# The last layer of a two-block model taken for its 256 real tokens instead of all 272

## What is computed

```python
h = jnp.concatenate([meta, x], axis=1)                      # 16 + 256 positions
...
def _diff_attend(qb, q_pos, kh, vh, k_pos, lam):
    s = jnp.einsum('bhcqd,bhckd->bhcqk', qb, kh)
    mask = k_pos[None, :] <= q_pos[:, None]
    p = jax.nn.softmax(jnp.where(mask, s, -jnp.inf), axis=-1)
    pd = p[:, :, 0] - lam * p[:, :, 1]
    return jnp.einsum('bhqk,bhkv->bhqv', pd, vh)
...
h = h + _diff_attn(hn, c_w_in[j], c_lambda[j], c_subln[j], c_w_out[j], lambda_init)
h = h + _sq_relu_mlp(_rmsnorm_2(h, norm_mlp[layer]), mlp_w1[layer], mlp_w2[layer])
...
h = _rmsnorm_2(h, norm_final)
return h[:, N_META:, :]
```

## Time and profile before

| | us |
|---|---|
| time, median of 3 runs | 2396.36 |
| lowest and highest of them | 2395.44, 2396.42 |
| span of the profiled execution | 2395.3 |
| PE busy in it | 2356.0 |
| DVE busy | 1701.0 |
| ACT busy | 1346.7 |

### The profile page before, as it was taken

How to read it: one execution, slowest core, us unless ns; L and a number is a source line. 1 busy time by engine, 2 the same in 40 slices (tenths; PEclk the granted TensorE clock), 3 DMA queues, 4 the chain that set the end, 5 groups by cost and what they waited for, 6 DMA issues and landing times.

```text
span 2395.3 us, 55555 instructions
## 1 busy us (share of the span) xinstructions
PE 2356.0 (98%) x20019; PEld 2260.4 (94%) x20019; DVE 1701.0 (71%) x3359; ACT 1346.7 (56%) x2806; POOL 3.4 (0%) x9
## 2 busy tenths in 40 slices
PE   8999999999999999999999999999999999999998
PEld 8899999789999999999998999999899999999998
DVE  7667667877658788776586677667666775677865
ACT  5555556365555555565555555557755454566443
POOL 0000000000000000000000000000000000000000
PEclk9999999999999999999999999999999999999999
DMA  6535665335654444456655356654444555434554
GB/s 240 176 118 169 195 204 167 96 110 181 204 177 133 138 134 140 141 167 193 201 165 178 124 167 193 201 172 151 140 129 143 167 177 178 130 112 142 176 183 132
DMA packets 103409, 385.88 MB, mean 161 GB/s; under 512 B 11345, under 2 KB 13521, under 8 KB 103025
## 3 DMA queue, kind: packets, MB, share of 16 engines
q1 hardware_dynamic: 102784, 381.78, 50.6%
q0 software_dynamic: 496, 2.38, 0.3%
HBM read 383.07 MB, written 1.05 MB: 160 GB/s over the span
## 4 chain that ended last, share of the span: by engine, by line
PE 87%; DVE 7%; ACT 3%; issue 2%; DMA 0%; DVEq 0%; ACTq 0%; SPq 0%
PE acc L533 25%; PE acc L540 24%; PE acc L539 24%; DVE weights_lo L2189 2%; PE acc L751 1%; PE acc L753 1%; PE acc L752 1%; ACT weights_hi L1334 1%; PE acc L773 1%; DVE h L2348 1%; DVE y L2337 1%; PE acc L840 1%; DVE xn_parts L2344 1%; PE acc L863 1%; PE acc L885 1%
## 5 line engine op out<-in xcount | busy, mean ns | idle before, releaser
L2189 DVE TENSOR_TENSOR weights_lo<-weights,weights_hi 128x512 fp32r<-128x512 f32 (+1 forms) x1160 | 754.4, 681 | 333.6 <-ACT weights_hi L1334 329.9
L1334 ACT ACTIVATE weights_hi<-weights 128x512 fp32r<-128x512 f32 (+1 forms) x1160 | 673.4, 618 | 189.7 <-PE acc L540 160.9
L533 PE MATMUL acc<-xn_parts,weights_hi 128*128 128x256 f32 (+1 forms) x2560 | 730.3, 285 | 8.7 <-DVE weights_lo L2189 7.1
L540 PE MATMUL acc<-xn_parts,weights_lo 128*128 128x256 f32 (+1 forms) x2560 | 719.4, 281 | 0.0
L539 PE MATMUL acc<-xn_parts,weights_hi 128*128 128x256 f32 (+1 forms) x2558 | 718.8, 281 | 0.0
L533 PEld LDWEIGHTS acc<-xn_parts,weights_hi 128*128 128x128 f32 x2560 | 482.2, 188 | 20.5 <-issue 10.7
L533 PE MATMUL acc<-arena_r,weights_hi 128*128 128x256 f32 (+1 forms) x1760 | 497.3, 283 | 3.0 <-DVE weights_lo L2189 1.7
L540 PE MATMUL acc<-arena_r,weights_lo 128*128 128x256 f32 (+1 forms) x1760 | 494.2, 281 | 0.0
L539 PE MATMUL acc<-arena_r,weights_hi 128*128 128x256 f32 (+1 forms) x1754 | 492.4, 281 | 0.0
L539 PEld LDWEIGHTS acc<-xn_parts,weights_hi 128*128 128x128 f32 x2558 | 481.0, 188 | 0.6
L540 PEld LDWEIGHTS acc<-xn_parts,weights_lo 128*128 128x128 f32 x2560 | 481.4, 188 | 0.0
(11 more groups left out here) (347 smaller groups left out, 2316.5 us busy)
## 6 DMA issues: line engine op xcount, KB each, us to landing
weights<-in_ffn_in SPq DMA_DIRECT2D x176, 512.0 KB, 4.1
weights<-in_ffn_out SPq DMA_DIRECT2D x64, 704.0 KB, 4.1
weights<-in_att_in SPq DMA_DIRECT2D x72, 512.0 KB, 3.6
weights<-in_mlp_in SPq DMA_DIRECT2D x64, 512.0 KB, 3.5
weights<-in_mlp_out SPq DMA_DIRECT2D x64, 512.0 KB, 3.6
weights<-in_ret_qk SPq DMA_DIRECT2D x32, 512.0 KB, 4.1
weights<-in_ret_v SPq DMA_DIRECT2D x32, 512.0 KB, 4.0
weights<-in_ret_g SPq DMA_DIRECT2D x32, 512.0 KB, 3.6
```

The costliest lines, as they stand in the source:

```text
L533: nc.tensor.matmul(acc, hi, src_hi, start=first, stop=False)
L540: return nc.tensor.matmul(acc, lo, src_hi, start=False, stop=last)
L1334: nc.scalar.activation(w_hi[phase.ring(sub)][:, 0:n, :], raw[slot][:, j * SUB:j * SUB + n, :], ACT.Copy)\
L2189: nc.vector.tensor_tensor(w_lo[phase.ring(sub)][:, 0:n, :], raw[slot][:, j * SUB:j * SUB + n, :], w_hi[phase.ring(sub)][:, 0:n, :].bitcast ...
```

## The change

In the last layer every width of 272 that belongs to queries, attention output, MLP and final norm becomes 256, the columns from position 16 on. Keys, values and their rotation stay 272 wide. The query tiles now begin at the first real token, two full tiles of 128 (`QUERIES`): the first sees 144 keys, the second 272. The third tile goes, with all of its steps on four engines (`block`, `last_scores`, `last_maxima`, `last_exp`, `last_weights`, `turn_last_p`). Since tiles of queries and of keys no longer begin at the same place, each query tile has 16 keys beyond its last full key tile: for them `turn_p` gets one small matmul a tile (16 columns of weights, 16 moving columns, L1116 of the new file), and `mix` takes them as two matmuls of 16 rows (L1140) where there was one.

```diff
+QUERIES = ((16, 144), (144, 272))
+COLUMNS2 = (S2, S1)
...
                 def rotate(i):
-                    for w in range(2):
-                        last = nc.tensor.matmul(PS[:, 2 + w, 0:S2], swap, proj2[:, i + (w * 8 - 1), :], start=True, stop=True)
-                    last.then_inc(A["rotated"], 1)
+                    nc.tensor.matmul(PS[:, 2, META:S2], swap, proj2[:, i - 1, META:S2], start=True, stop=True)
+                    nc.tensor.matmul(PS[:, 3, 0:S2], swap, proj2[:, i + 7, :], start=True, stop=True).then_inc(A["rotated"], 1)
...
+                        at = (2 * st + (u - st)) * P
+                        nc.tensor.transpose(PS[:, 6, at:at + P], c_pd[:, u, st * P:(st + 1) * P], ident)
+                    keys, at = slice((u + 1) * P, (u + 1) * P + META), 3 * P + u * META
+                    nc.tensor.matmul(PS[0:META, 6, at:at + META], c_pd[:, u, keys], ident[:, P - META:P], start=True, stop=True)\
+                        .then_inc(A["p_turned"], 1)
...
-                    for st, (s0, sl) in enumerate(TILES2):
-                        last = nc.tensor.matmul(PS[:, 7, s0:S2], c_vn[0:sl, st, :], c_pt[0:sl, st, s0:S2],
-                                                start=(st == 0), stop=(st == 2))
+                    nc.tensor.matmul(PS[:, 7, 0:S1], c_vn[:, 0, :], c_pt[:, 0:S1], start=True, stop=False)
+                    nc.tensor.matmul(PS[:, 7, P:S1], c_vn[:, 1, :], c_pt[:, S1:S1 + P], start=False, stop=False)
+                    for u in range(2):
+                        last = nc.tensor.matmul(PS[:, 7, (u + 1) * P - META:(u + 1) * P], c_vn[0:META, u + 1, :],
+                                                c_pt_tail[0:META, u * META:(u + 1) * META], start=False, stop=(u == 1))
...
+                    if u < 0:
+                        multiply(phase, i, u, PS[:, 0, 0:S1], tokens)
+                    else:
+                        multiply(phase, i, u, PS[:, (u + 1) % 2, 0:S2], src)
...
-                    last_scores(i)
...
-                last = product(PS[:, o, 0:S2], w_hi[after.ring(sub)][:, n, :], w_lo[after.ring(sub)][:, n, :],
+                last = product(PS[:, o, 0:S1], w_hi[after.ring(sub)][:, n, :], w_lo[after.ring(sub)][:, n, :],
...
-                dense_outputs(ph[f"mlp_in{layer}"], src, S2, ready)
-                post_sum(17 + 2 * layer, S2)
-                src, ready = hidden(mlp_hi, mlp_lo, f"mlp_in{layer}")
-                dense_outputs(ph[f"mlp_out{layer}"], src, S2, ready)
+                n = COLUMNS2[layer]
+                src, ready = normed(2 * DEPTH + 2 * layer + 1, n)
+                dense_outputs(ph[f"mlp_in{layer}"], src, n, ready)
+                post_sum(17 + 2 * layer, n)
+                src, ready = hidden(mlp_hi[:, :, 0:n], mlp_lo[:, :, 0:n], f"mlp_in{layer}")
+                dense_outputs(ph[f"mlp_out{layer}"], src, n, ready)
...
-                    nc.vector.tensor_tensor(part[:, u % 2, :], silu[:, u % 2, :], silu[:, u % 2, :], ALU.mult).then_inc(part_ready, 1)
+                    nc.vector.tensor_tensor(part[:, u % 2, 0:n], silu[:, u % 2, 0:n], silu[:, u % 2, 0:n], ALU.mult).then_inc(part_ready, 1)
```

More of the change, by code:

```diff
@@ L160, in constants @@
     second["causal_T"] = np.concatenate([np.where(r > pos, BIG, 0.0) for r in row], 1)
-    second["causal"] = np.concatenate([np.where(pos > r, -BIG, 0.0) for r in row[:2] + [TILES2[2][0] + p[:, None] % 64]], 1)
-    second["both"] = (p[:, None] % 64 == np.arange(META)[None, :]) * 1.0
+    second["causal"] = np.concatenate([np.where(pos > t0 + p[:, None], -BIG, 0.0) for t0, _ in QUERIES], 1)
     sel = np.zeros((P, A_HEADS * P))
@@ L1105, in scores @@
                 def scores(i):
                     pe.wait_ge(A["roped"], i)
-                    for u, (t0, tl) in enumerate(TILES2[:2]):
+                    for u, (t0, t1) in enumerate(QUERIES):
                         for e in range(2):
                             rows = slice(64 * e, 64 * e + 64)
-                            acc = (PS[:, 2 + e, 0:P], PS[:, 2 + e, P:P + S1])[u]
-                            last = nc.tensor.matmul(acc, c_q[rows, t0:t0 + tl], c_k[rows, 0:t0 + tl], start=True, stop=True)
+                            last = nc.tensor.matmul(PS[:, 2 + e, u * QUERIES[0][1]:u * QUERIES[0][1] + t1],
+                                                    c_q[rows, t0:t1], c_k[rows, 0:t1], start=True, stop=True)
@@ L1163, in mean_square, with tokens, project @@
                     pe.wait_ge(A["squares_ready"], i - 2)
-                    nc.tensor.matmul(PS[:, 5, 0:S2], mean, c_sq, start=True, stop=True).then_inc(A["sum_ready"], 1)
-                def project(i, u, ready=None):
+                    nc.tensor.matmul(PS[:, 5, 0:S1], mean, c_sq, start=True, stop=True).then_inc(A["sum_ready"], 1)
+                def tokens(k):
+                    return tuple(part[:, META:S2] for part in src(k))
+                def project(i, u):
                     pe.wait_ge(out_evacuated, i * NU + (FREE_BANKS + phase.out0 + (u if u < 1 else 0)))
-                    multiply(phase, i, u, PS[:, (u + 1) % 2, 0:S2], src, ready)
+                    if u < 0:
+                        multiply(phase, i, u, PS[:, 0, 0:S1], tokens)
+                    else:
+                        multiply(phase, i, u, PS[:, (u + 1) % 2, 0:S2], src)
                 def turn(i, weigh, norm):
@@ L2421, in rest @@
                         .then_inc(x_split, 1)
-                sum_squares(k, phase, S2, unit, rest if scaled_by else None, late=True, ahead=ahead)
+                sum_squares(k, phase, n, unit, rest if scaled_by else None, late=True, ahead=ahead)
             def last_attention_to_h():
@@ L3411, in _ @@
             last_attention_to_h()
-            square_relu(ph["mlp_in1"])
+            square_relu(ph["mlp_in1"], S1)
             add_to_h(20, ph["mlp_out1"], factor=True)
```

200 lines of the change are left out of this document (66 added, 134 removed).

## The result

| | before | after |
|---|---|---|
| time, median (4 runs each, same chip), us | 2396.39 | 2381.36 |
| lowest and highest | 2395.44, 2396.61 | 2380.63, 2382.63 |
| profiled execution, span | 2395.3 | 2380.0 |
| `mlp_out1`, first to last product | 94.80 | 87.12 |
| `mlp_in1`, first to last product | 96.12 | 92.12 |

The ratio is 0.9939, 95% interval 0.9927 to 0.995. The time lies in the predicted range (2373.0 to 2382.0), 4.4 above the predicted 2377.0. In the spans the change is 15.3: 0.04 up to the first rotation, 2.53 between the rotations, 1.05 to the start of `mlp_in1`, 4.0 in it, 7.68 in `mlp_out1`, nothing in the tail (9.05 both times).

The account below looks back on a forecast made before the run. PE was taken to bound the kernel, with DVE or ACT right behind it in places. Gains of 7.7 + 3.6 + 1.0 + 0.5 + 1.5 + 5.0 + 0.15 = 19.4 took 2396.4 to 2377.0 us, range 2373.0 to 2382.0.

Parts of the forecast that it names:

- `mlp_out1`, 7.7: mlp_out1: PE alone sets the time; 768 matmuls gain 10.0 ns each at the fast pace, 7.7 us.
- The rival had 0.25: mlp_out1: matmuls run at the slow pace, 117.8 ns, so 3.4 us less gained, 2380.4; chance 0.25.
- `mlp_in1`, 3.6: mlp_in1: a loop over PE, ACT and DVE limits the unit period to 2.85 from 2.97; thirty periods gain 3.6 us.
- the loop doesn't bind: mlp_in1: PE's own 2.72 a unit holds, gaining 7.5 us instead of 3.6, total 2373.1; chance 0.10.
- the first-to-second start at about 0.22 in nearly every unit: mlp_in1: expected trace sign of the binding loop, beside ReLU to ReLU of 2.84 to 2.88; 0.11 would mean no bound.
- `c_out` and the way in, 1.5: c_out to mlp_in1's first unit: 1.0 us from c_out's first 96 matmuls, 0.5 from the rest beside a DVE/ACT chain.
- a wait above 0.72: Before mlp_in1's second unit: PE's 0.72 us wait for weights_lo was expected to grow.
- Query units, 1.5: Query units: 192 matmuls, each unit behind an interruption, gain 7.9 ns each at a mixed pace of 115.5; 1.5 us.
- The steps between a head's units, 5.0: Head turns: 8.9 gone and 0.8 narrower, less 0.4 wider scores, 2.7 turn_p and 1.6 mix; 5.0 us (2.2 to 6.9).
- one whose stored side has only 16 columns should be below that. 0.085 x 4: turn_p: its two new small matmuls take four passes below 0.115 each, at 0.085, costing 2.7 us over 8 heads.
- Slower by the clock: mlp_in1: PE's waits drop the clock to 1.2 GHz; 2454 if all 768 products run there; chance of slower 0.02.
- the new small matmuls cost what they replace: turn_p and mix: passes at 0.19 cost 9.1 us instead of 4.3, total 2381.8; chance 0.08, shared with another wait.

Follow-up runs that it names:

- e10: e9 with the new weight order also in mlp_in0, the 272-column layer before the last; 2373.25 us, ratio 0.99.
- e12: e10 with the first half of the weights of mlp_in1's second unit split one step earlier; 2374.48 us, ratio 0.9911.
- e1: Changed kernel, in mlp_in1 the first half of unit u+2's weights split ahead of unit u's ReLU and square; 2377.47 us, ratio 0.9923.
- e2: Kernel before the change, with the same new order in mlp_in1 as e1; 2396.24 us, ratio 0.9998.
- e3: Kernel before, with 256 columns only in c_out, mlp_in1, mlp_out1 and final norm, attention as before; 2384.0 us, ratio 0.9948.
- e7: Changed kernel, query units reading columns 0 to 255 instead of 16 to 271 (wrong tokens, timing only); 2380.66 us, ratio 0.9933.
- e8: Changed kernel, one hi x lo matmul of each query unit issued as two halves of 128 columns; 2382.56 us, ratio 0.9942.
- e4: Changed kernel, turn_p's two small matmuls as transposes of 32 queries x 16 keys; 2382.90 us, ratio 0.9941.
- e6: Changed kernel, turn_p's small matmuls as transposes over 128 queries and mix's two 16-row matmuls over 128 rows with zeros; 2378.03 us, ratio 0.9924.
- e9: Changed kernel with the edits of e1 and e6 together; 2374.38 us, ratio 0.9914.

## Why the prediction was right, and where it was off

- **`mlp_out1`, 7.7:** measured 7.68, the fast pace. In all twelve kernels that take 256 columns there it took 87.12 to 87.13, in e10 and e12 too, where `mlp_in1` ran slow. The rival had 0.25; nothing here supports it for this stage. The gain per product is 10.0 ns, as the rows had it; the Trainium skill's gap of N/2.4 + 2.5 ns ("TensorE: Matmul & The Clock Gate", Back-to-back issue gap), which the page gives for an isolated matmul, would make it 6.7 and the stage's gain 5.1, and the measurement speaks against it for this dense stream.
- **`mlp_in1`, 3.6:** measured 4.0, at a mean period of 2.849 (forecast 2.85). e1 and e2 show that the loop binds, and that before the change it cost 0.4 at most; so the rival "the loop doesn't bind" falls. Wrong was "the first-to-second start at about 0.22 in nearly every unit": it is every second one, presumably since a unit that was late gives the next its weights in time.
- **`c_out` and the way in, 1.5:** 0.91 to the start of `mlp_in1` and 1.01 to its second unit (e3). The 10 ns a product came (four of `c_out`'s units at 0.1178, two at 0.1134, 0.1257 before), but more of it went into waits than I counted: 1.13 us from start to start before the second unit, 1.01 before. The expected sign, a wait above 0.72, is there as 0.85:

```profile
2195.20 0.39 PE L530 MATMUL acc<-xn_parts,weights_hi 128*128 128x256 f32 x1 [0.85 <-DVE weights_lo L2152]
```

- **Query units, 1.5:** 0.09 instead of 0.19 a turn, 0.7. The step that failed is "at a mixed pace of 115.5": it was 120 ns, because of where the columns begin (e7, e8).
- **The steps between a head's units, 5.0:** the term that was mis-sized most. What goes was right (1.11 a turn), and so were the scores (0.05) and `mix` (0.17 in all; forecast 0.20 for the new matmul less 0.05 for the narrower ones). The step that failed is "one whose stored side has only 16 columns should be below that. 0.085 x 4": per turn 0.62 instead of 0.34, above my upper bound of 0.14 a pass. I priced the passes themselves, 0.04 and 0.11 of them from start to start. The price lies in the starts around them, where the loads aren't made ahead (e4 to e6). The one narrower step that stands apart, the rotation, gained 0.02 as forecast; `mean_square` became 0.09 longer instead of 0.03 shorter. And in the first turn nothing stands behind the last unit once `last_scores` is gone, so that PE waits for ACT there and the turn gains only 0.08 (11.86 to 11.78). Against that, the 0.3 less to wait for `c_in`'s first weights is in no term:

```profile
2071.87 0.28 PE L537 MATMUL acc<-xn_parts,weights_lo 128*128 128x272 f32 x1
2072.64 0.39 PE L530 MATMUL acc<-xn_parts,weights_hi 128*128 128x256 f32 x1 [0.49 <-ACT arena L2010]
```

- **Slower by the clock:** the waits of `mlp_in1` did nothing to the clock; it was granted 1.00 from 1687.8 to the end of `mlp_out1`. But the clock does fall elsewhere: at 1684.4 in the changed kernel's execution, in code that the change doesn't touch (1.12 us lost), and in e6, e9 and e10 at the entry to `c_in`, just behind a PE wait of 1.57.
- **Tail, 0.15:** nothing.

The rival "the new small matmuls cost what they replace" thus has a share: 0.62 a turn in `turn_p` against its 0.76 and my 0.34, but 0.17 in `mix` against its 0.38. Its 2381.8 lies close to the measured 2381.36 only because other misses (the first turn, the query units, the way into `mlp_in1`) fill the sum up.

That the time fell into the range is in part luck. 2381.36 lies in the stretch from 2379.2 to 2381.8, which the prediction had put in for the slow pace in `mlp_out1`. That pace did not come; an attention that gave half of its 6.5 did, at the low side of the 2.2 to 6.9 that were allowed for its steps. The terms of the MLP, 11.7 of the 15.3, were right by their mechanism and their size.

## To carry over

Price a small matmul by what it does to the loads around it: of the steps tried here, one that keeps all 128 rows and 128 moving columns, zeros or unused ones included, cost less than one cut to what is needed. When a stage gets shorter on the engine that bounds it, look for the loop over the other engines that stood just behind, and check whether half of next unit's preparation can be put ahead of this unit's last steps. And where an edit takes the waits out of a long stretch of 256-column products, look at the pace it enters with: in e10 and e12 it held to the stage's end, and was fast again in the next stage. Before a difference of 1 to 3 us is read from the total, compare the granted clock of both executions over their whole length.
